# The second block's input chunks in a new order, with its attention head by head between the contraction steps of the spatial gate's chunks

## The reference

```
h = rms_norm(x, norm1_g) * (1 + scale1) + shift1
proj = h @ w_in                                   # 2048 -> 5 * 512
u_a, v_a, q, k, v = jnp.split(proj, SPLIT_POINTS, axis=-1)
y_a = chunked_spatial_gating(u_a, v_a, ...)       # gelu both, norm v_a, u * (tril(ws) @ v + bs) in chunks of 128 tokens
q = rms_norm(q.reshape(B, S, 4, 128), q_norm_g)
k = rms_norm(k.reshape(B, S, 4, 128), k_norm_g)
y_b = stick_breaking_attention(q, k, v)           # 4 heads of 128, strictly causal
y = rms_norm(concatenate([y_a, y_b]) in 8 groups of 128, out_norm_g)
x = x + gate1 * (y @ w_out)                       # 1024 -> 2048
h = rms_norm(x, norm2_g) * (1 + scale2) + shift2
x = x + gate2 * hierarchical_moe(h, ...)          # routing, then only the chosen experts
```

## Time and profile before

| what | value |
|---|---|
| median of 3 runs | 2384.46 us (2382.83 to 2385.02) |
| the profiled execution, own time | 2385.41 us |
| its span in the trace | 2383.3 us |
| mean granted TensorE clock | 0.932 of full speed |
| PE busy | 2065.4 us, 87% |
| DVE, ACT, POOL busy | 795.7, 360.5, 176.2 us |

### The profile page before, as it was taken

The page is one execution under the profiler, slowest core; times in us unless marked ns, Lnnn a source line. Parts: engine busy times, 40 slices in busy tenths (PEclk is TensorE's granted clock), DMA queues, the critical chain, the costliest instruction groups (busy, mean ns, idle before and its releaser), DMA issues.

```text
span 2383.3 us, 20347 instructions
## 1 busy us (share of the span) xinstructions
PE 2065.4 (87%) x7709; PEld 1080.7 (45%) x7709; DVE 795.7 (33%) x1247; ACT 360.5 (15%) x680; POOL 176.2 (7%) x242
## 2 busy tenths in 40 slices
PE   7999999999999999999999997598557777877871
PEld 3444545444544554444444445444534444444441
DVE  0266534240583544453320003313212222222223
ACT  0011231210400231002400013202001110110110
POOL 0000031000000000010000000000111111111101
PEclk9999999999999999999999998799578899888986
DMA  6885633152135438671232211020389999999995
GB/s 229 354 346 196 228 133 115 53 211 71 36 103 207 148 106 321 223 275 40 71 106 71 80 62 35 27 71 0 133 332 421 420 421 420 421 421 419 421 421 230
DMA packets 120118, 500.51 MB, mean 210 GB/s; under 512 B 17446, under 2 KB 17724, under 8 KB 76156
## 3 DMA queue, kind: packets, MB, share of 16 engines
q1 hardware_dynamic: 86556, 316.37, 34.6%
q0 software_dynamic: 22864, 128.29, 14.3%
q10 hardware_dynamic: 10640, 55.07, 5.7%
HBM read 456.65 MB, written 43.04 MB: 210 GB/s over the span
## 4 chain that ended last, share of the span: by engine, by line
PE 70%; DMA 21%; DVE 4%; ACT 2%; issue 1%; POOL 1%; SPq 0%; ACTq 0%; POOLq 0%; DVEq 0%
PE bank L770 38%; DMA RM<-in_w_up 17%; PE bank L773 12%; PE bank L992 6%; PE bank L800 5%; PE bank L669 2%; DMA RG<-in_w_mod 2%; PE bank L950 1%; PE bank L846 1%; PE bank L910 1%; DMA RX<-ys_d,sli 1%; PE bank L719 1%; PE bank L706 1%; PE bank L679 1%; DMA RH<-in_x 1%
## 5 line engine op out<-in xcount | busy, mean ns | idle before, releaser
L770 PE MATMUL bank<-RW,RX 128*128 128x512 f32 (+1 forms) x1792 | 740.5, 573 | 14.3 <-ACT RM L1019 6.1
L770 PEld LDWEIGHTS bank<-RW,RX 128*128 128x128 f32 x1792 | 330.5, 191 | 409.7 <-issue 404.1
L992 PE MATMUL bank<-RX,RG 128*64 128x256 f32 x1088 | 291.2, 435 | 99.3 <-DMA RM<-in_w_up 96.5
L773 PE MATMUL bank<-RX,RW 128*128 128x512 f32 x768 | 341.7, 599 | 4.4 <-ACT RA L1019 4.4
L992 PE MATMUL bank<-RM,RG 128*64 128x256 f32 x1088 | 291.9, 435 | 0.0
L992 PEld LDWEIGHTS bank<-RX,RG 128*64 128x64 f32 x1088 | 168.9, 158 | 204.6 <-issue 154.1
L1381 DVE SCALAR_TENSOR_TENSOR RG<-RG,ccol 128x2048 f32<-128x2048 f32 x90 | 212.0, 2355 | 142.6 <-DMA RG<-in_w_mod 136.5
L773 PEld LDWEIGHTS bank<-RX,RW 128*128 128x128 f32 x768 | 145.2, 193 | 173.1 <-issue 170.8
L992 PEld LDWEIGHTS bank<-RM,RG 128*64 128x64 f32 x1088 | 168.8, 158 | 0.0
L770 PE MATMUL bank<-RW,RM 128*128 128x512 f32 x384 | 165.8, 593 | 0.9 <-PE bank L770 0.6
L1019 ACT ACTIVATE RA<-bank 128x512 f32<-128x512 f32 (+1 forms) x170 | 87.8, 563 | 392.3 <-PE bank L679 111.5
(11 more groups left out here) (215 smaller groups left out, 1568.5 us busy)
## 6 DMA issues: line engine op xcount, KB each, us to landing
RG<-in_w_mod POOLq DMA_DIRECT2D x96, 1024.0 KB, 5.2
RW<-in_w_in SPq DMA_DIRECT2D x72, 1024.0 KB, 5.1
RX<-in_w_gate SPq DMA_DIRECT2D x34, 2048.0 KB, 20.7
RM<-in_w_up SPq DMA_DIRECT2D x34, 2048.0 KB, 25.3
RW<-in_w_down SPq DMA_DIRECT2D x34, 2048.0 KB, 26.4
RW<-in_w_out SPq DMA_DIRECT2D x24, 1024.0 KB, 5.3
ys_d<-RA ACTq DMA_DIRECT2D x68, 256.0 KB, 6.7
ys_d<-RM ACTq DMA_DIRECT2D x1, 16384.0 KB, 71.7
```

The lines of the kernel that those rows point to most:

```text
L770: ins = nc.tensor.matmul(banks[j][:, 0:width], act[:, ka, j * P:(j + 1) * P], W[:, s, kt % 4, 0:width], start=kt == 0, stop=kt == kk - 1)
L773: ins = nc.tensor.matmul(banks[j][:, :], W[:, s, kt % 4, j * P:(j + 1) * P], act[:, kt, :], start=kt == 0, stop=kt == kk - 1)
L992: ins = nc.tensor.matmul(ps[2][lo:lo + 64, 0:256], xgT[u][:, j, h, :], w[:, h, j, :], start=h + j == 0, stop=h + j == 8)
```

## The change

Four things change together.

- The chunks of the second block's input go q2, k2, v2, va, ua. `out2` follows in the same stage, so that the two barriers around the attention are gone (`PH_MOE` counts them).
- The attention stands in `beside`, counted in steps t from the start of va (0 to 15 in va, 16 to 31 in ua). For head h = 0, 1, 2, 3 the scores come behind t = 1, 7, 13, 19, the sums behind 5, 11, 17, 24, the values behind 7, 13, 19, 26, the head's four transposes behind 11, 17, 23, 30; the spatial gate's matmuls behind 31. The other 16 transposes come behind the fourth step of `out2`, whose contraction starts with the attention's half (rows 512 to 1023 of w_out).
- The norm of the attention's output goes head by head (`take_values`, `head_root`, `scale_head`), that of the spatial gate's on its own (`gate_spatial`).
- Buffers move, since X must stay whole in RX: one set of softplus buffers in RG and RA in place of two in RX, `yT` in RM over q and k, `gate` in RG. A head's scores take banks 4 to 6, the fourth block of 128 columns in a free corner of bank 5. The second gate vector is loaded later and awaited before the expert loop.

```diff
-        yT = RX[:, 0:4096].rearrange("p (k t) -> p k t", k=8)
+        yT = RM[:, 0:4096].rearrange("p (k t) -> p k t", k=8)
...
-        SPall, ATall, EAall = ([RX[:, b + TRI * w:b + TRI * (w + 1)] for w in range(2)] for b in (0, 2 * TRI, 4 * TRI))
+        SPall, EAall, ATall = RG[:, 0:TRI], RG[:, 3648:3648 + TRI], RA[:, 4096:4096 + TRI]
...
-        chunks += [(k, w_in2, c, 512, 16, True) for k, c in (("va", 512), ("ua", 0), ("q2", 1024), ("k2", 1536), ("v2", 2048))]
+        chunks += [(k, w_in2, c, 512, 16, True) for k, c in (("q2", 1024), ("k2", 1536), ("v2", 2048), ("va", 512), ("ua", 0))]
...
-        STAGES = [list(range(0, 18)), list(range(18, 23)), list(range(23, 27))]
+        STAGES = [list(range(0, 18)), list(range(18, 27))]
...
+        SB_AT = first["va"]
+        SCORES_AT, LOGA_AT, SUMS_AT, HEAD_AT, SPATIAL_AT = {1: 0, 7: 1, 13: 2, 19: 3}, {5: 0, 11: 1, 17: 2, 24: 3}, {7: 0, 13: 1, 19: 2, 26: 3}, {11: 0, 17: 1, 23: 2, 30: 3}, 31
+        GATED2_AT = (first["out2"], 3)
...
-                    at = 4 * ((q + 2) % 4) if kind == "out" else 4 * q
+                    at = 4 * ((q + 2) % 4) if kind == "out" else 4 * ((q + 1) % 2) if kind == "out2" else 4 * q
...
+                    values(SUMS_AT[t])
+                if t in SCORES_AT:
+                    scores(SCORES_AT[t])
+                if t in LOGA_AT:
+                    log_a(LOGA_AT[t])
+                if t in HEAD_AT:
+                    h = HEAD_AT[t]
+                    pe.wait_ge(sem("head_ready"), h + 1)
+                    transposes(("yT", h), [Y[:, tt, 512 + h * P:512 + (h + 1) * P] for tt in range(TT)])
+                if t == SPATIAL_AT:
+                    spatial()
+                if (c, kt) == GATED2_AT:
+                    pe.wait_ge(sem("spatial_ready"), 1)
+                    for g in range(4):
+                        transposes(("yT", 4 + g), [Y[:, tt, g * P:(g + 1) * P] for tt in range(TT)])
...
+                    if c == first["out2"]:
+                        pe.wait_ge(*freed(("yT", kt)))
...
+            def soften(h):
+                act.wait_ge(sem("abs_ready"), h + 1)
+                fn(EAall, EAall, ACT.Exp)
+                st.settle()
+                fn(EAall, EAall, ACT.Ln, sem("log_ready"), bias=1.0)
...
+                    if c == SB_AT:
+                        store_gates()
+                        soften(0)
+                        weigh(0)
+                        soften(1)
+                        head_root(0)
+                        weigh(1)
+                        take_head(0)
+                        soften(2)
+                        head_root(1)
+                        work(c)
+                        weigh(2)
+                        take_head(1)
+                        va_root()
+                        continue
+                    if c == SB_AT + 1:
+                        soften(3)
+                        head_root(2)
+                        take_head(2)
+                        weigh(3)
+                        act.wait_ge(sem("gate_stored"), 32)
+                        act.dma_start(gate, bcast_row(gates_d[0])).then_inc(sem("gate_landed"), 16)
+                        head_root(3)
+                        take_head(3)
+                        work(c)
+                        gated2()
+                        continue
...
+            def negative_abs(h):
+                if h:
+                    dve.wait_ge(sem("log_a_ready"), 4 * h)
+                for j in (0, 1, 3, 2):
+                    ts(tri(SPall, j), zbank(h, j), 0.0, None, ALU.max)
+                st.settle()
+                for j in (0, 1, 3, 2):
+                    stt(tri(EAall, j), tri(SPall, j), -2.0, zbank(h, j), ALU.mult, ALU.add)
+                st.settle()
+                dve.sem_inc(sem("abs_ready"), 1)
+            def softplus(h):
+                dve.wait_ge(sem("log_ready"), h + 1)
+                tt_(SPall, SPall, EAall, ALU.add)
+                st.settle()
+                for j in range(4):
+                    part = tri(SPall, j)[:, 0:P]
+                    tt_(part, part, C["before"], ALU.mult)
+                st.settle()
+                dve.sem_inc(sem("fail_ready"), 1)
+            def take_values(h):
+                key = ("O", h)
+                bk = filled(dve, key)
+                y = Y[:, :, 512 + h * P:512 + (h + 1) * P]
+                st.do(v.tensor_copy(y, bk[:, :].rearrange("p (t d) -> p t d", t=TT)), *freed(key))
+                dve.wait_ge(*freed(key))
+                tt_(hsq, y, y, ALU.mult)
+                st.settle()
+                st.do(v.tensor_reduce(ss[:, 16 + 4 * h:20 + 4 * h], hsq, AX.X, ALU.add))
+                st.settle()
+                inv_mean(rs[:, 16 + 4 * h:20 + 4 * h], ss[:, 16 + 4 * h:20 + 4 * h], P, 1e-6, sem("head_mean"))
+            def scale_head(h):
+                dve.wait_ge(sem("head_root"), h + 1)
+                y = Y[:, :, 512 + h * P:512 + (h + 1) * P]
+                tt_(y, y, per(rs[:, 16 + 4 * h:20 + 4 * h], [P, TT, P]), ALU.mult, sem("head_ready"))
+            def va_mean():
...
+            def gate_spatial():
+                dve.wait_ge(sem("copied"), 10)
+                for tt in range(TT):
+                    key = ("SPG", tt)
+                    bk = filled(dve, key)
+                    for g in range(4):
+                        cols = slice(g * P, (g + 1) * P)
+                        stt(Y[:, tt, cols], bk[:, cols], pack[:, 98 + g:99 + g], UA[:, tt, cols], ALU.add, ALU.mult,
+                            *(freed(key) if g == 3 else (None, None)))
+                for tt in range(TT):
+                    dve.wait_ge(*freed(("SPG", tt)))
+                ya = Y[:, :, 0:512]
+                tt_(SQ, ya, ya, ALU.mult)
+                st.settle()
+                st.do(v.tensor_reduce(ss[:, 0:16], SQ[:, :, :].rearrange("p t (h d) -> p (t h) d", d=P), AX.X, ALU.add))
+                st.settle()
+                inv_mean(rs[:, 0:16], ss[:, 0:16], P, 1e-6, sem("mean_ready"))
+                dve.wait_ge(sem("root_ready"), 4)
+                for tt in range(TT):
+                    x = Y[:, tt, 0:512].rearrange("p (h d) -> p h d", d=P)
+                    tt_(x, x, per(rs[:, 4 * tt:4 * tt + 4], [P, 4, P]), ALU.mult)
+                st.settle()
+                dve.sem_inc(sem("spatial_ready"), 1)
...
+                    if c == SB_AT:
+                        negative_abs(0)
+                        softplus(0)
+                        negative_abs(1)
+                        take_values(0)
+                        softplus(1)
+                        scale_head(0)
+                        negative_abs(2)
+                        take_values(1)
+                        softplus(2)
+                        scale_head(1)
+                        va_mean()
+                        continue
+                    if c == SB_AT + 1:
+                        negative_abs(3)
+                        va_scale()
+                        take_values(2)
+                        softplus(3)
+                        scale_head(2)
+                        take_values(3)
+                        scale_head(3)
+                        gate_spatial()
+                        continue
```

More of the change, by code:

```diff
@@ L428, in program @@
             if n == 1:
[L429 to L438, removed]
                 for kt in range(KD):
@@ L720, in values_of, with zbank, scores @@
                 full(ins, ("PV", u))
-            def beside(c, kt):
+            def zbank(h, j):
+                bk = ps[use["Z", h, (0, 1, 2, 1)[j]][0]]
+                return bk[:, 384:512] if j == 3 else bk[:, 0:S - P * j]
+            def scores(h):
+                if h == 0:
+                    for jj in range(4):
+                        pe.wait_ge(*freed(("T", first["q2"], jj)))
+                        pe.wait_ge(*freed(("T", first["k2"], jj)))
+                for j in range(3):
+                    claim(("Z", h, j))
+                for j in (0, 1, 3, 2):
+                    ins = nc.tensor.matmul(zbank(h, j), kT2[:, h, j * P:(j + 1) * P], qT2[:, h, j * P:S], start=j != 3, stop=True, skip_group_check=True)
+                    if j != 1:
+                        full(ins, ("Z", h, (0, 1, 2, 1)[j]))
@@ new lines, in log_a @@
+            def log_a(h):
+                pe.wait_ge(sem("fail_ready"), h + 1)
+                for j in (0, 1, 3, 2):
+                    bk = zbank(h, j)
+                    n = S - P * j
+                    for jj in range(j, 4):
+                        nc.tensor.matmul(bk[:, (jj - j) * P:n], C["neg_from"] if jj == j else C["neg_ones"], tri(SPall, jj),
+                                         start=False, stop=False, skip_group_check=True)
+                    ins = nc.tensor.matmul(bk[:, 0:P], ident, C["not_before"], start=False, stop=True, skip_group_check=True)
+                    ins.then_inc(sem("log_a_ready"), 1)
@@ new lines, in values, with spatial @@
+            def values(h):
+                pe.wait_ge(sem("a_ready"), h + 1)
```

(24 more changed lines are left out.)

219 lines of the change are left out of this document (68 added, 151 removed).

## The result

The changed kernel took **2345.32 us** (median of 4 runs, 2343.81 to 2349.04) against 2383.76 us (4 runs, 2382.83 to 2385.02): a ratio of 0.9841, with its 95% interval from 0.9828 to 0.9855. Forecast were 2342.5 us and 2336 to 2351. The profiled execution took 2345.02 us, with a span of 2343.0 us at a mean granted clock of 0.941.

The account below looks back on a forecast made before the run. TensorE's chain bounds the stretches before the expert loop, with a 95.66 us hole at the attention. 96.26 us becoming 54.3 gains 42.0: 2385.41 to 2343.4 profiled, 2342.5 as median; range 2336 to 2351.

Parts of the forecast that it names:

- The place and the gain: From v2's end to out2's first step: 96.26 us before, 54.3 after, a gain of 42.0 us.
- the hole: The attention's stretch between the v chunk's last matmul (1442.44 us) and out2 (1538.10): 95.66 us, no projection beside it.
- my terms: From v2's end to out2's end: 54.3 us for all but projections, plus 2 x 55.17 and out2's 112.
- The chains: A head's scores to masks on DVE and ACT take 11.1 us; PE comes at 15.9, slack 4.8; head 3 has 0.8.
- Rival 3: The head chains don't fit: a wait ahead of each head's sums or transposes, 17 us, so 2359; chance 0.12.
- (a): Boundary v2 to va: va starts 3.85 us after v2's end, the 1.94 us of transposes inside.
- (b): Boundary va to ua: PE waits 2.7 us for ACT's table loads, root and gelu, plus 1.5 us for clock and late banks.
- Rival 2: No wait at all at va to ua, or the clock holds: 2.7 + 1.5 us less, 2338.3; chance 0.12.
- The spatial gate: After ua: DVE done at E + 13.6, PE back from four out2 steps at E + 17.7; 4 us left.
- rival 4: A drain beside each ACT table load: the va to ua wait is 3.8 us longer, time 2346.3; chance 0.05.
- rival 5: PE's clock falls to its lower level through va, ua and the attention: 156 us more, 2498; chance 0.03.
- Everything after them moves as a block: Everything behind out2's four chunks keeps its length; out2's end to span's end is the same within 2 us.

## Why the prediction held, and where it was off

- **The place and the gain.** Right: the hole was the stretch to fill, and filled it gives its length less the moved work. The 276.6 us of my terms measured 276.65.
- **The chains.** Right: 11.13 us against 11.1 for heads 0 to 2. For head 3, S being the start of its scores, DVE ends head 2's scaling at S + 15.1 as forecast (1451.32), 0.8 us before PE comes for it (1452.11), with no idle on PE:

```profile
1436.21 2.32 PE L742 MATMUL bank<-RM 128*128 128x512 f32 x8
...
1450.63 0.69 DVE L1427 TENSOR_TENSOR RM<-RM,rs 128x512 f32<-128x512 f32 x1
...
1452.11 0.60 PE L676 MATMUL bank<-cst,RM 128*128 128x128 f32 x4
```

  Rival 3 is out. When the slack was taken away, the waits came (5.5 and 8.6 us), and 1.5 to 2.3 us of clock behind each.
- **(a) v2 to va.** 4.03 us from v2's end to va's start against 3.85: the wait was 1.78, where 0.30 and 1.94 off my 3.85 leave 1.6.
- **(b) va to ua.** The sum has 2.7 us for the wait and 0.3 for the boundary, 3.0 together, and the profile's 3.05 holds both. The clock behind it cost 8.65 - 7.11 = 1.54 us against 1.5. The order of ACT and the step of the scores each move it as the sum says. Rival 2 did not come by itself; one step of a table makes it.
- **The spatial gate.** Forecast 4 us of cover. DVE's scaling ended at 1501.88 and PE came at 1505.77: 3.9. With three steps fewer it waits 6.37.

```profile
1499.38 2.50 DVE L1427 TENSOR_TENSOR RM<-RM,rs 128x512 f32<-128x512 f32 x4 [0.28 <-ACT rs L1039]
...
1505.77 1.91 PE L676 MATMUL bank<-cst,RM 128*128 128x128 f32 x16
```

- **The drain, rival 4.** Out. ACT's next function starts 0.01 to 0.02 us after each load's end, and the wait with three loads is 0.05 us over my sum, not 3.8. The Trainium skill's page "ScalarE: Activation LUTs" (section "What ACT_TABLE_LOAD costs") adds a drain of 1380 ns to each switch; no profile here shows it.
- **The clock in va and ua, rival 5.** Out: 0.99.
- **"Everything after them moves as a block"** is the step that was off, and with it the sign that out2's end to the end of the span would stay the same within 2 us: it grew by 4.2. The steps behind out2 took 106.4 us instead of 102.4. Of these 4.0 us, 3.2 are the transposes and the router (36.1 against 32.9), and the rest is a longer wait for DMAs (41.90 against 41.17 us).
- **The time came out closer than the terms, by luck.** Against the 4.0 us lost, out2's end came 2.5 us sooner than my sum put it: 1.1 from before the k2 chunk, and 1.4 since the v chunk ran 55.46 us behind the wait of 2.27 where it had taken 56.87. Both move between executions of the same code. In all the profiled execution gained 40.4 us where I had 42.0, and the median of its runs 38.4.

What the 3.1 us behind out2 are can be read from the granted clock over 16 us that take in the change of level in both (columns as in the earlier trace rows; the last but two is the clock). The changed kernel first, then the one with ACT's order changed:

```profile
1618.00:1634.00 16.00, 15.04 (x96) 14.88 (x94) 5.67 (x7) 6.86 (x9) 0.00 (x0) 0.71 0.44 183
```

```profile
1618.00:1634.00 16.00, 15.04 (x111) 14.88 (x110) 4.86 (x7) 6.73 (x8) 0.00 (x0) 0.82 0.52 214
```

In every profile without added work there, the clock is at the lower level (1.2 GHz, 0.50) where the transposes start, behind 9.8 us of idle, goes up to 2.4 GHz while they run, and falls back in the router's matmuls. A mean of 0.71 is 6.7 us of the 16 at the upper level, 0.82 is 10.2. All three profiles of the changed kernel have 0.71 over such 16 us, and the two of the kernel before and those of the kernels that add no work there have 0.82. So the two behind out2 lose 3.1 us because the clock stays up about 3.5 us less. What decides between the two lengths is **open**. The code there is the same, and so is the idle ahead of the transposes, 9.8 us. The kernels that shorten or remove ua's wait have 33.0, and so have the two that add waits of their own. I have no run that sets the arrival at this place alone.

## What to carry to other kernels

Where one engine idles for a chain on others and has independent steps of known length, price a chain from its start to its last result, put the consumer that many steps behind plus a spare one, and check the queue of every engine at the nearest chunk boundary: there the moved work stands ahead of the bank's takeover, and its order or one step of distance was worth 3 to 4 us here, where a head's chain without its cover cost 5.5 us and more. Transposes that delay the takeover of a chunk's banks are better moved inside the next chunk (4.7 us here). And a sum over TensorE's work is good to 3 or 4 us in such a kernel, for the clock behind each wait isn't the sum's to give.

## What the runs showed of the hardware that I had not expected

- The same idle of 2.27 us ahead of a chunk is followed by 55.46 us in some executions, at a granted clock of 1.00, and by 56.9 in others, at 0.97 (55.46 in the first profile of the changed kernel, 56.92 in the next, same code). Behind 3.05 us of idle 16 matmuls took 8.57 to 8.80 us instead of 7.11; behind 1.54 and 1.78 us they lost nothing.
- A wait can cost less than its length, and a gain less than it seems: 64 transposes and 128 matmuls some 120 us behind took 33.0 or 36.1 us, with nothing changed in them, by whether the clock stayed up for about 10.2 or 6.7 us. A kernel with 8 us more of waits was only some 3 us slower.
- The router's 128 small matmuls took 23.2 to 26.2 us in all runs. With 7 to 11 us of matmuls and then the transposes at the full clock just ahead of them it was 25.0 to 26.0, so more work ahead did not keep the clock up through them.
